# One head's recurrence in a hybrid decoder step: small matmuls gathered into one block per step, sample update ahead of the output

## The reference, cut to what matters

```
q_dec = q * exp(bcum);  k_intra = k * exp(-bcum);  k_state = k * exp(blast - bcum)
att = where(causal, q_dec @ k_intra^T, 0)
o = att @ v + q_dec @ S
S = exp(blast) * S + k_state^T @ v            # chunk by chunk for the prompt
S_sample[b] = exp(blast_b) * S_sample[b] + k_state_b^T @ v_b     # once for each of 8 samples
o = o * rsqrt(mean(o*o) + eps) * norm_g * silu(z);  y = o @ w_out
```

## Time and profile before

| | us |
|---|---|
| median of 3 runs | 1720.27 |
| lowest and highest | 1717.53, 1724.99 |
| the profiled execution | 1722.27 |
| its span, first to last instruction | 1720.5 |
| TensorE busy in it | 1644.9 (96%) |
| VectorE, ScalarE, GpSimd busy | 833.3, 483.5, 397.3 |

### The profile page before, as it was taken

How to read it: one execution, slowest core, us unless ns; L and a number is a source line. 1 busy time by engine, 2 the same in 40 slices (tenths; PEclk the granted TensorE clock), 3 DMA queues, 4 the chain that set the end, 5 groups by cost and what they waited for, 6 DMA issues and landing times.

```text
span 1720.5 us, 26408 instructions
## 1 busy us (share of the span) xinstructions
PE 1644.9 (96%) x10307; PEld 1564.1 (91%) x10307; DVE 833.3 (48%) x1245; ACT 483.5 (28%) x1021; POOL 397.3 (23%) x392
## 2 busy tenths in 40 slices
PE   6899999999999999997999999999999999999997
PEld 3798999999999999996898899988999889998896
DVE  4494439453844475456224561235621456324465
ACT  4321112110211111134335403264132532225423
POOL 3221212121221212113224121232112331213310
PEclk8999999999999999997999999999999999999999
DMA  9322211221222122210112211122111221111212
GB/s 352 129 62 72 75 44 55 74 76 39 67 76 62 53 66 71 67 27 26 37 38 75 80 39 50 37 62 80 51 38 37 62 92 38 41 47 38 98 43 104
DMA packets 145621, 115.23 MB, mean 67 GB/s; under 512 B 5885, under 2 KB 128345, under 8 KB 145506
## 3 DMA queue, kind: packets, MB, share of 16 engines
q1 hardware_dynamic: 143680, 112.87, 21.3%
q10 hardware_dynamic: 1834, 0.74, 0.2%
HBM read 99.05 MB, written 15.00 MB: 66 GB/s over the span
## 4 chain that ended last, share of the span: by engine, by line
PE 88%; DVE 8%; ACT 2%; issue 1%; DMA 1%; SPq 0%; POOL 0%; ACTq 0%; DVEq 0%
PE psA L515 45%; PE psB L515 29%; PE psB L1774 2%; PE psB L1791 2%; PE psX L1756 2%; DVE PQ L1273 2%; PE psB L1782 1%; PE psX L1811 1%; DMA ada<-in_ada_w 1%; PE psB L1823 1%; DVE y_rows L1523 1%; PE psX L1636 1%; DVE a_hi L591 1%; ACT PQ L1049 1%; DVE ksm L1418 1%
## 5 line engine op out<-in xcount | busy, mean ns | idle before, releaser
L322 POOL TENSOR_TENSOR w_lo<-stage,w_hi 128x1024 fp32r<-128x1024 f32 x112 | 279.0, 2492 | 1059.4 <-ACT w_hi L317 1059.4
L515 PE MATMUL psA<-h_hi,w_hi 128*128 128x362 f32 (+1 forms) x1152 | 277.4, 350 | 24.5 <-DVE h_lo L453 15.3
L515 PE MATMUL psA<-h_lo,w_hi 128*128 128x362 f32 (+1 forms) x1152 | 256.9, 332 | 0.0
L515 PE MATMUL psA<-h_hi,w_lo 128*128 128x362 f32 (+1 forms) x1152 | 255.6, 330 | 0.0
L515 PEld LDWEIGHTS psA<-h_hi,w_hi 128*128 128x128 f32 x1152 | 202.4, 192 | 53.5 <-issue 48.3
L317 ACT ACTIVATE w_hi<-stage 128x1024 fp32r<-128x1024 f32 x112 | 120.1, 1072 | 392.3 <-PE psB L515 301.3
L515 PEld LDWEIGHTS psA<-h_lo,w_hi 128*128 128x128 f32 x1152 | 204.2, 193 | 0.0
L515 PEld LDWEIGHTS psA<-h_hi,w_lo 128*128 128x128 f32 x1152 | 203.4, 192 | 0.0
L515 PE MATMUL psB<-h_hi,w_hi 128*128 128x362 f32 (+1 forms) x576 | 129.1, 332 | 1.7 <-ACT kT L1049 1.7
L515 PE MATMUL psB<-h_hi,w_lo 128*128 128x362 f32 (+1 forms) x576 | 126.3, 327 | 0.0
L515 PE MATMUL psB<-h_lo,w_hi 128*128 128x362 f32 (+1 forms) x576 | 126.2, 327 | 0.0
(11 more groups left out here) (314 smaller groups left out, 2369.7 us busy)
## 6 DMA issues: line engine op xcount, KB each, us to landing
stage<-in_gla_w_in SPq DMA_DIRECT2D x40, 512.0 KB, 3.9
stage<-in_pool_w_in SPq DMA_DIRECT2D x32, 512.0 KB, 4.1
ada_stage<-in_ada_w SPq DMA_DIRECT2D x24, 512.0 KB, 3.5
ada<-in_ada_w SPq DMA_DIRECT2D x8, 1024.0 KB, 12.2
stage<-in_pool_w_out SPq DMA_DIRECT2D x16, 512.0 KB, 3.5
v<-in_state_gla SPq DMA_DIRECT2D x32, 256.0 KB, 2.6
out_new_gla_sample<-v SPq DMA_DIRECT2D x32, 256.0 KB, 2.1
stage<-in_gla_w_out SPq DMA_DIRECT2D x16, 512.0 KB, 3.6
```

The source lines that it names most:

```text
L322: nc.gpsimd.tensor_tensor(w_lo[:, j % 2, :], stage[:, j % 2, :], w_hi[:, j % 2, :].bitcast(f32), ALU.subtract).then_inc(lay.lo_done, 1)
L515: last = nc.tensor.matmul(ps[u][:, t, 0:width], weight(w[:, p, :], k), a[:, k, n0:n0 + width], start=(k == 0 and pas == 0), stop=(k == kt ...
```

## The change

TensorE's step is put in another order. Before: one part of the fill, `scores`, `key_rows`, `output`, `update`, another part, `mean_square`, `sample_inter`, `sample_update`. After: `scores`, `key_rows`, `sample_inter`, `sample_update`, `output`, `mean_square`, `update`, and then both parts of the fill together. Six parts instead of seven lie before step 0. VectorE makes the masked keys of a sample a step earlier, as the last thing in its step, and `sample_state` moves ahead of `scale_qk`. On ScalarE `gate_in(0)` and `gate_in(1)` come a step later, and `gate_in(2)` comes behind the copy of `smp_rows`. Two waits take the counts of the new order, and one wait for the evacuation of Z2 is added ahead of the count of `unit_done`. GpSimd's and SyncE's programs stay as they are.

```
-FILL_START, FILL_STEP = 7, 2
+FILL_START, FILL_STEP = 6, 2
  (ScalarE)
                 for s in range(NSUP):
-                    if s in (0, 4):
+                    if s in (1, 5):
                         gate_in(s // 4)
...
-                gate_in(2)
                 act.wait_ge(smp_rows_done, g + 1)
                 nc.scalar.activation(smp_rows, X[1], ACT.Copy).then_inc(smp_rows_out, 1)
+                gate_in(2)
                 split_slot(L1, GP, act, g, GP.slot["O01"])
                 o_out(NSUP)
  (VectorE)
                 for s in range(NSUP + 2):
-                    if s >= 2:
-                        ks_rows(s - 2)
                     if s + 1 < NSUP:
                         att_out(s + 1)
                     if s + 2 < NSUP:
                         qd_args(s + 2)
+                    if s >= 2:
+                        sample_state(s - 2)
+                    if s + 2 < NSUP:
                         scale_qk(s + 2)
                     if s < NSUP:
                         state(s)
                     if s + 1 < NSUP:
                         scale_qs(s + 1)
-                    if s >= 2:
-                        sample_state(s - 2)
+                    if 1 <= s <= NSUP:
+                        ks_rows(s - 1)
  (TensorE, update)
-                    if s >= 3:
-                        pe.wait_ge(s0_ready, g * NB + s - 2)
+                    if s >= 2:
+                        pe.wait_ge(s0_ready, g * NB + s - 1)
  (TensorE, sample_update)
-                    if b + 2 < NSUP:
-                        pe.wait_ge(S_ready, g * NSUP + b + 3)
+                    if b + 2 <= NSUP:
+                        pe.wait_ge(S_ready, g * NSUP + b + 2)
  (TensorE, the steps)
                 for s in range(NSUP + 2):
-                    if s <= NSUP:
-                        fill(1)
                     if s + 1 < NSUP:
                         scores(s + 1)
                         key_rows(s + 1)
+                    if s in (2, 4, 6, 8):
+                        sample_inter(s - 2)
+                    if s >= 2:
+                        sample_update(s - 2)
                     if s < NSUP:
                         output(s)
-                        update(s)
-                        fill(FILL_STEP - 1)
                     if 1 <= s <= NSUP:
                         pe.wait_ge(att_ready, g * NSUP + min(s + 2, NSUP))
                         mean_square(s - 1)
-                    if s in (2, 4, 6, 8):
-                        sample_inter(s - 2)
+                    if s < NSUP:
+                        update(s)
                     if s == NSUP + 1:
                         sample_out()
-                    if s >= 2:
-                        sample_update(s - 2)
+                    if s <= NSUP:
+                        fill(FILL_STEP)
+                pe.wait_ge(L1.evac[0], evacs(GP, g, GP.unit["Z2"]))
                 pe.sem_inc(L1.unit_done, 1)
```

## The result

The changed kernel takes 1733.25 us (median of 4 runs, 1729.53 to 1734.25), the kernel before 1721.08 beside it: the ratio is 1.007, with an interval of 1.0053 to 1.0086. Run again beside other kernels it took 1732.19 us against 1721.26, a ratio of 1.0066 (1.0052 to 1.008). The change costs 11 to 12 us. The forecast was 1729.6, slower by 9.3.

What follows compares the result with a forecast made beforehand. TensorE, busy 96% of the span, was taken as the bound, so only its standing or half clock counts. Terms -7.3 + 5.8 + 10.8 + 0 = +9.3 us gave 1729.6 us on the median; range 1716 to 1739.

Steps and rivals of the forecast that it cites:

- The old wait goes: TensorE's wait for the masked keys (L1418), once per head, ends because they are made a step earlier: -7.3 us.
- The start wait: At each head's second scores, TensorE waits 1.45 us for decayed keys, one fill part lying between instead of three: +5.8 us.
- The tail wait: At the samples' mean square, TensorE waits 2.7 us per head for GpSimd's L892, behind the gate products: +10.8 us.
- L890 and L892 need 0.8 us from T + 7.3: At the tail, GpSimd's two instructions start only after both gate products; the sum is ready at T + 8.1.
- The sum by the letter: Lock rule read literally: GpSimd enters after the first gate product at T + 6.0, L892 ends about T + 8.0.
- The joints: Joining small matmuls in the steps changes which weight loads hide behind long matmuls: 0, within 3.2 us either way.
- The clock: Half clock behind tail waits costs the same 7.8 us as before, none behind start waits: term 0.
- The third rival: The clock falls at both waits of each head: +17.1 us, 1737.4 us; chance 0.13.
- The first rival: GpSimd is not kept out at the tail, so only the start wait stays: -8.3 us, 1712.0 us; chance 0.15.
- The second: Rival: the change does only what its order says, no new wait opens: -15.1 us, 1705.2 us; chance 0.04.
- The fourth: Rival: sample states land late, step 8 waits 0.5 us more per head: 1731.8 us, or 1738; chance 0.08.

Runs made afterwards that it cites:

- both waits gone: Changed kernel with one part of the fill moved behind the first scores and GpSimd's square sum ahead of its low half for O01: 1708.87 us, ratio 0.9933.
- the old order without these waits: Kernel before with only GpSimd's square sum of the samples moved ahead of its low half for O01: 1705.23 us, ratio 0.9912.
- taking the start wait out of the changed kernel: Changed kernel with one part of the fill moved from ahead of V's last transposes to behind the first scores: 1720.78 us, ratio 1.0003.
- mending its tail: Changed kernel with GpSimd's square sum of the samples ahead of its low half for O01 in step 8: 1717.68 us, ratio 0.9979.
- the run with the products waiting: Changed kernel, GpSimd's order kept, VectorE waiting for the samples' square sum before the first gate product: 1717.17 us, ratio 0.9983.

## Why the prediction was right, and where its terms were off

The direction, the two new waits and their places were as forecast, and the time fell inside the range and inside the forecast's own range of 1723 to 1736. That the total came so close, 9.3 against 10.9 and 12.2 us, is in part luck: the two new waits were put 2.3 us too long together, and two terms that were put at nothing cost 5 to 6. Term by term:

- **The old wait goes, -7.3 us.** Right: no line for L1418, which ends at 959.75, before L1824 is due at 961.42.
- **The start wait, +5.8.** It is 5.1: 1.28 us per head instead of 1.45. The step that was off is the arrival of TensorE. I let the fill end after 1.5 us, the distance to the start of the next matmul, while the wait is counted from the modelled end of the last one, here 1118.89 (1120.18 - 1.29) and 1.74 us after the fill's start.
- **The tail wait, +10.8.** It is 9.2, 2.3 per head. The step that failed is "L890 and L892 need 0.8 us from T + 7.3". With T = 961.42, the start of the sample's update, L322 ends at T + 4.8 as worked out, but L890 ends at 967.70, T + 6.3, over a microsecond before both products are over (968.85), and L892 at T + 7.6. The two products taken one by one (shortest/median/longest ns, first and last start), the first head of the changed kernel and then all of the kernel before:

```profile
L1432 DVE SCALAR_TENSOR_TENSOR oT<-oT,vecT,PQ x2: 1536/2090/2645, 964.7 to 967.3; 128x1088 f32<-128x1088 f32 x2
L1432 DVE SCALAR_TENSOR_TENSOR oT<-oT,vecT,PQ x12: 1344/1350/1353, 966.9 to 1648.4; 128x1088 f32<-128x1088 f32 x12
```

The first ends at 967.39 (964.74 + 2.65), the second takes 1.54 us where one takes 1.35 undisturbed, and L890 ends in between, 0.31 us behind the first and 1.15 ahead of the end of the second. It is so in all four heads, to 0.01 us. So GpSimd was let in behind the first product, as far as ends on GpSimd can be trusted, and it cost the second 0.2 us. That is how the Trainium skill's rule (SBUF — State Buffer, "SBUF: two separate sides") reads by the letter, and the trace agrees with it here more than with the earlier trace rows, from which I chose; why GpSimd did not get in between the two VectorE instructions there, if it did not, stays open. The sum by the letter, T + 8.0, was still too late by 0.4: L890 cost the second product 0.2 us and not its own half microsecond, and L892 ended 0.18 us behind that product, where it takes 0.32 alone.

- **The joints, 0 with 3.2 either way.** With both waits gone the changed order still takes more. A head of that kernel is 84.23 us with one more part of the fill in it (1.49), so 82.74, where a head of the old order without these waits is 82.25: 0.5 per head, +2.0 us. That difference is measured; where it arises I read from the traces only, and no run separates it. In the chain of waits L1792 takes 0.97 us behind L1847, where L1791 took 0.86 behind `output`; that its weight load has no long matmul to hide behind is my reading, not shown. The shorter L1824 in steps without `sample_inter` (0.23 against 0.34) gives back only a part.
- **The clock, 0.** Here the sum was short. I let the tail waits cost what the old one did and the start waits nothing, by the four waits of 1.5 us that kept the clock at 1.00. The tail part held in the second trace: 0.17 + 0.34 + 0.17 + 0.17 of four stretches of 10 us are 8.5 us, against 7.8; in the first, three of the four waits took the clock down. The start part did not: of the 24 start waits in the six profiled executions that have them, ten took the clock to half, at 0.16 x 11 = 1.8 us each. The third rival, with 0.13, was thus half true. The two traces of the changed kernel show the clock's cost by itself: their waits are equal, 9.2 and 5.1 us, but the heads took 352.6 us in the one with four half-clock stretches and 357.0 in the other with six, one of them twice as long.

The terms as measured are -7.3 + 5.1 + 9.2 + 2.0, which is 9.0, and some 3 to 4 us of clock: 12 to 13, where 10.9 and 12.2 were measured in the two comparisons. By medians, taking the start wait out of the changed kernel gives 11.4 us and mending its tail 14.5, but both together 23.3. The three kernels and the changed one were not all run in one set, and single runs of one kernel spread over 3 to 8 us, so 2 or 3 us between these sums say nothing. The 10.2 us for the start wait are its 5.1, some 3 us of clock at ten falls in 24 waits, and 2 us that stay unexplained within that spread.

The first rival, that GpSimd is not kept out, is settled by the run with the products waiting: 7.9 of the 9.2 us are the hold. The second, that no new wait opens, is refuted by the two new lines. The fourth, late sample states, did not come up in the changed kernel; no wait for that load is listed.

What stays open is why a wait of 1.3 us at the start of a head takes the clock down in some heads and executions, while the four waits of 1.5 us in the first layer did so in none of the twelve traces. Short matmuls stand around the first and long ones around the second, but no run here changed that by itself.

## What to carry to other kernels

When a wait ends in a collision of two engines, look at what both have next before moving the victim: here the keys were moved out of the way and the next two VectorE instructions with both operands in SBUF were hit, at a place where TensorE waited for what GpSimd had queued behind. The repair was to put the short result that TensorE wants ahead of the long one that nobody needs yet, in the program of the engine that did both; it gave 15.7 us with no change to TensorE's order. A fill that is moved is also taken from somewhere: count what each part of it covered, by the chain that runs beneath it.

## What the runs showed of the hardware

A wait of TensorE costs more than its length where the clock falls behind it. In this kernel the waits of 1.8 us took it down in 11 of 12 cases, those of 2.3 us in 13 of 16, those of 1.3 us in 10 of 24, for 1.7 us or so of work each time, and in two of these 34 falls for about twice as much (0.71 and 0.66 over 10 us). With only the four waits of 0.8 us ahead of the samples' scores left in the heads, it stayed at 1.00 over 760 us. VectorE's instructions with two operands in SBUF and GpSimd's stood for each other by nearly the whole length of what was running: 0.35 us became 2.47, and GpSimd's add of 0.32 us became 1.25. A GpSimd instruction that stood was let in between two VectorE instructions queued back to back, in four heads of four. `sample_state`, which reads one operand from PSUM, took 0.73 to 0.75 us in every place, and in each trace of the changed kernel 12 of its 32 ran beside an instruction of GpSimd.
